# Attention probabilities transposed through device memory instead of on TensorE

## The chip, the cores and the metric

The kernel runs on one core of one Trainium2 chip. The metric is the device time of one execution in microseconds (us). Three executions of the kernel before gave 814.75, 814.80 and 814.91 us, median 814.8 us.

## What is computed

Two layers of a hybrid decoder trunk on 256 tokens of width 2048, all in float32. Each layer normalizes x, multiplies it with one wide input matrix (2048 x 6232), runs four mixers on the result, and multiplies their gated outputs with an output matrix (2048 x 2048):

```python
for l in range(DEPTH):
    h = _rmsnorm(x, ln_g[l])
    u = h @ w_in[l]
    y_a = _gla(...) * silu(g_a)
    y_b = _ssd_mixer(...)
    y_c = _mla(...) * silu(g_c)             # causal attention, 4 heads
    y_d = _dilated_attention(...) * silu(g_d)   # attention on dilated windows, 4 heads
    x = x + concatenate([y_a, y_b, y_c, y_d]) @ w_out[l]
```

The change concerns the two attentions, `mla` and `dil`. For each head: scores s = q k^T * scale with a mask, p = softmax(s), output p v. To multiply with v, TensorE needs the probabilities p with the keys on the partitions, and the softmax leaves them with the queries on the partitions: they have to be transposed.

## The kernel before

**The stream.** The large multiplications run as a stream of 148 units a layer: 144 units of two 128-row slabs of a weight block (`STREAM`, blocks of up to 512 columns, eight units each) and 4 projection units. Float32 weights are split into a high and a low float32r part. For each unit SP loads the weights into `raw` (four buffers, L530), ACT makes `w_hi` (L1019), DVE makes `w_lo` (L1384), and TensorE does 12 matmuls (hi x hi, hi x lo at L705 and L706, lo x hi at L714). `w_hi` and `w_lo` have four buffers each: ACT may split unit n once TensorE has finished unit n-4, and SP loads the weights of unit n once DVE has split unit n-4.

**The jobs.** The mixers' small TensorE work is put between the units. `PE_AT` names the unit behind which each job runs: `mla S 0: 89`, `mla PT 0: 92`, `mla S 1: 93`, `mla O 0: 94`, `mla PT 1: 96`, `mla O 1: 98`, `dil S 0: 99`, `dil PT 0: 102`, `dil S 1: 103`, `dil O 0: 104`, `dil PT 1: 106`, `dil O 1: 108`, `yT 3: 114`. The names `0` and `1` are pairs of heads. S is the scores, PT the transposition of the probabilities, O the product with the values. Jobs take turns on two halves of a PSUM tensor (`pairs`), and each waits for the last reader of the job two before it (`LAST_READER`).

**ACT and DVE** walk through the same units. At unit n each first does its split of unit n and then the work hung on that number: DVE takes the maximum of the scores at the unit of S plus 3 (`smax`, L1675, into `Pb`), ACT takes the exponential there (`probs`, L1221), then TensorE transposes `Pb` (`probs_T`, L899), ACT copies PSUM to `PT` (L1227), TensorE multiplies with the values (`values`, L910 to L912), and DVE scales the result by the sums (`out_heads`, L1707). For `dil` DVE also multiplies the probabilities with the tap counts (`taps`, L1687). The order of all signalling steps of each engine is written out in `ORDER`. A step that waits holds up everything behind it on its engine, the splits of later units too.

**Squares.** Seven other transpositions a layer (`SQUARES`: `ssd x`, `ssd y`, `dil q`, `dil k`, `y 0`, `y 1`, `y 2`) use no TensorE. DVE transposes 32 x 32 squares (`turn_squares`, L1353), one DMA writes the 512 KB to device memory (`squares_out`, L512), and when that has landed four DMAs read them back so that the squares take their new places (`squares_back`, L519). SP issues these DMAs in its queue among the weight loads, the first 5 units and the others 7 units behind the number in `SQUARES`. GpSimd does eight small reciprocal square roots a layer (`rsqrt`, L613 and L615) and four small loads.

Of the kernel before, what the change touches and what calls it, by code (L numbers as in the profile page):

```python
# [187 lines left out]
for _n in range(8):  # L188
# [3 lines left out]
          "mla kv 1": KV_AT, "ssd Y": 76, "mla qT": 85, "mla kT": 86, "mla rT": 87, "mla S 0": 89, "mla PT 0": 92,  # L192
          "mla S 1": 93, "mla O 0": 94, "mla PT 1": 96, "mla O 1": 98, "dil S 0": 99,
          "dil PT 0": 102, "dil S 1": 103, "dil O 0": 104, "dil PT 1": 106, "dil O 1": 108,
# [9 lines left out]
for _m in ("mla", "dil"):  # L204
    for _i in range(2):
        LAST_READER |= {f"{_m} S {_i}": ("dve", f"{_m} max {_i}"), f"{_m} PT {_i}": ("act", f"{_m} PT {_i}"),
                        f"{_m} O {_i}": ("dve", f"{_m} O {_i}")}
# [24 lines left out]
        "mla S 0, mla PT 0, mla S 1, mla O 0, mla PT 1, mla O 1, dil S 0, dil PT 0, dil S 1, dil O 0, "  # L232
        "dil PT 1, dil O 1, yT 3",
# [6 lines left out]
        "mla rT, mla P 0, ssd rs sum, mla PT 0, mla P 1, evac 11, mla PT 1, dil q, dil P 0, dil PT 0, "  # L240
        "evac 12, dil P 1, dil PT 1, yT 0, yT 1, yT 2, evac 13, yT 3",
# [8 lines left out]
        "mla nmax 0, dil q squares, dil k squares, mla max 1, mla nmax 1, y 1, mla ri 0, mla O 0, y 1 squares, y 0, y 0 squares, mla ri 1, mla O 1, dil max 0, "  # L250
        "dil nmax 0, dil P 0, dil max 1, dil nmax 1, dil P 1, dil ri 0, dil O 0, y 2, y 2 squares, yT 0, dil ri 1, dil O 1, yT 1, "
        "yT 2, y 3, yT 3, x turn 0, x turn 1, x turn 2",
# [7 lines left out]
def build(nc, xT_d, x_d, pos_d, cols_d, w_d, params_d, gla_w2, gla_b,  # L260
          consts_d, masks_d, out_d):
    ctx = ExitStack()
    with ctx:
# [117 lines left out]
        SQUARES["dil k"] = A(6656, 1024), A(6656, 1024), 93  # L381
# [69 lines left out]
        squares_d = {name: nc.dram_tensor(name.replace(" ", "_") + "_squares", (P, 4 * S), F32, kind="Internal").ap() for name in SQUARES}  # L451
# [55 lines left out]
        def _(sp):  # L507

            def squares_out(l, name):

                sp.wait_ge(*reached("dve", l)(f"{name} squares"))
                sp.dma_start(squares_d[name], SQUARES[name][0]).then_inc(squares_out_done[name], 16)  # L512

            def squares_back(l, name):

                sp.wait_ge(squares_out_done[name], 16 * (l + 1))
                away, to = squares_d[name].rearrange("(i b) (f c) -> f b i c", b=32, f=4), SQUARES[name][1]
                for f in range(4):
                    sp.dma_start(to[32 * f:32 * f + 32].rearrange("b (i c) -> b i c", i=4), away[f]).then_inc(squares_in[name], 16)  # L519
# [1358 lines left out]
```

## Time and profile before

| | us |
|---|---|
| median of three executions | 814.8 |
| profiled execution: its own time | 815.04 |
| profiled execution: span from first to last instruction | 813.2 |
| TensorE busy in it | 806.8 |
| DVE busy in it | 613.7 |
| ACT busy in it | 473.7 |
| share of the 16 DMA engines busy, mean | 64% |

The span is 1.8 us shorter than the execution's own time. Busy times overlap. The profile lists for each instruction its start, duration, source line and what ended the idle time before it; TensorE's unit boundaries are read off the start of the first L705 matmul of each unit.

### The profile page before, as it was taken

How to read it: one execution, taken by the hardware profiler on the slowest of the kernel's cores; microseconds unless marked ns; L12 is line 12 of the kernel's file. 1: busy time of each engine (PE TensorE's matmuls, PEld its weight loads, DVE VectorE, ACT ScalarE, POOL GpSimd, SP SyncE). 2: the span in 40 equal slices, each digit the busy share in tenths (PEclk: the TensorE clock that was granted, in tenths of full speed). 3: DMA queues.
4: the chain of work that ended last, by engine and by line, in shares of the span. 5: the costliest groups of instructions: out<-in, count | busy, mean ns of one | idle time of the engine just before them, and what ended most of it. 6: DMA issues, size and time to landing. Idle time of an engine off the chain costs nothing.

```text
span 813.2 us, 11261 instructions
## 1 busy us (share of the span) xinstructions
PE 806.8 (99%) x4164; PEld 684.3 (84%) x4164; DVE 613.7 (75%) x1092; ACT 473.7 (58%) x784; POOL 60.1 (7%) x64
## 2 busy tenths in 40 slices
PE   8999999999999999999999999999999999999998
PEld 5888887999887888888888888889998888888886
DVE  6678899877898766678964967979779977665452
ACT  6566544866965666433556465447687565664331
POOL 7100000110401000000000000003014010000000
PEclk9999999999999999999999999999999999999999
DMA  9956634586676967656576655355767677666553
GB/s 328 347 217 207 186 133 159 135 246 193 200 246 206 240 225 232 200 175 205 165 260 183 195 161 186 111 168 151 239 203 234 209 226 249 194 222 215 188 193 118
DMA packets 57687, 165.67 MB, mean 204 GB/s; under 512 B 6624, under 2 KB 14480, under 8 KB 57632
## 3 DMA queue, kind: packets, MB, share of 16 engines
q1 hardware_dynamic: 57120, 164.67, 63.9%
q8 instruction: 33, 0.54, 0.3%
q10 hardware_dynamic: 320, 0.21, 0.1%
q14 instruction: 22, 0.18, 0.1%
q0 software_dynamic: 192, 0.07, 0.1%
HBM read 155.47 MB, written 9.45 MB: 203 GB/s over the span
## 4 chain that ended last, share of the span: by engine, by line
PE 91%; DVE 6%; issue 2%; DMA 1%; ACT 0%; SPq 0%; DVEq 0%; ACTq 0%
PE gemm L705 27%; PE gemm L714 27%; PE gemm L706 26%; DVE arena L1345 3%; DVE w_lo L1384 2%; PE pairs L885 1%; PE pairs L855 1%; PE pairs L860 1%; PE pairs L856 1%; PE pairs L826 1%; PE pairs L771 1%; DVE arena L1473 1%; PE pairs L868 1%; PE pairs L899 1%; DMA u<-in_xT_dram 1%
## 5 line engine op out<-in xcount | busy, mean ns | idle before, releaser
L1384 DVE TENSOR_TENSOR w_lo<-raw,w_hi 128x1024 fp32r<-128x1024 f32 (+2 forms) x295 | 324.4, 1109 | 146.0 <-ACT w_hi L1019 144.3
L705 PE MATMUL gemm<-w_hi,a_hi 128*128 128x512 f32 (+1 forms) x1144 | 420.8, 373 | 0.3 <-ACT w_hi L1019 0.3
L706 PE MATMUL gemm<-w_hi,a_lo 128*128 128x512 f32 (+1 forms) x1144 | 414.3, 368 | 0.0
L1019 ACT ACTIVATE w_hi<-raw 128x1024 fp32r<-128x1024 f32 (+2 forms) x295 | 281.5, 968 | 214.1 <-PE gemm L714 137.0
L714 PE MATMUL gemm<-w_lo,a_hi 128*128 128x512 f32 (+1 forms) x1144 | 281.7, 368 | 0.2
L705 PEld LDWEIGHTS gemm<-w_hi,a_hi 128*128 128x128 f32 x1144 | 215.2, 188 | 36.4 <-issue 2.1
L706 PEld LDWEIGHTS gemm<-w_hi,a_lo 128*128 128x128 f32 x1144 | 215.2, 188 | 33.1
L714 PEld LDWEIGHTS gemm<-w_lo,a_hi 128*128 128x128 f32 x1144 | 203.2, 188 | 36.5 <-DVE w_lo L1384 1.9
L613 POOL TENSOR_TENSOR st<-st,powers 128x4 f32<-128x4 f32 (+2 forms) x8 | 10.1, 1263 | 429.5 <-ACT arena L1100 212.5
L1052 ACT ACTIVATE u<-gemm,st 128x512 f32<-128x512 f32 (+1 forms) x40 | 22.1, 603 | 15.8 <-PE gemm L714 15.8
L1221 ACT ACTIVATE arena<-arena,st 128x128 f32<-128x128 f32 (+1 forms) x32 | 13.1, 444 | 30.9 <-DVE st L1679 30.9
L1345 DVE STREAM_TRANSPOSE arena<-u 32x256 f32<-32x256 f32 x64 | 27.9, 436 | 1.2
L1345 DVE STREAM_TRANSPOSE u<-x 32x256 f32<-32x256 f32 x48 | 20.9, 436 | 0.6
L1554 DVE SCALAR_TENSOR_TENSOR u<-arena,allp,u 128x256 f32<-128x256 f32 x48 | 20.9, 473 | 0.0
L1202 ACT ACTIVATE arena<-u 128x192 f32<-128x192 f32 (+1 forms) x64 | 20.6, 335 | 0.0
L1644 DVE SCALAR_TENSOR_TENSOR u<-u,sth,param_rows 128x192 f32<-128x192 f32 (+1 forms) x64 | 19.9, 376 | 0.0
L1083 ACT ACTIVATE arena<-arena 128x256 f32<-128x256 f32 x16 | 6.8, 423 | 18.0 <-DVE arena L1445 18.0
L1675 DVE CUSTOM_DVE_ANT_0 arena<-pairs,cst 128x128 f32<-128x128 f32 (+1 forms) x32 | 9.5, 352 | 8.5 <-issue 3.5
L771 PEld LDWEIGHTS pairs<-arena 128*128 128x128 f32 x112 | 14.7, 191 | 1.2
L1513 DVE COPY_PREDICATED o<-lmask,pairs 128x512 f32<-128x512 uint8 x14 | 12.4, 886 | 4.2 <-issue 4.2
L1336 DVE SCALAR_TENSOR_TENSOR a_lo<-u,allp,a_hi 128x256 fp32r<-128x256 f32 x28 | 14.2, 552 | 1.6 <-ACT a_hi L1000 1.5
L771 PE MATMUL pairs<-arena 128*128 128x128 f32 x112 | 14.8, 275 | 0.0
(201 smaller groups left out, 623.3 us busy)
## 6 DMA issues: line engine op xcount, KB each, us to landing
raw<-in_weights_dram SPq DMA_DIRECT2D x225, 512.0 KB, 4.3
raw<-in_weights_dram SPq DMA_DIRECT2D x64, 278.0 KB, 3.1
y_squares<-arena SPq DMA_DIRECT2D x6, 512.0 KB, 6.0
arena<-y_squares SPq DMA_DIRECT2D x24, 128.0 KB, 3.9
raw<-in_weights_dram SPq DMA_DIRECT2D x6, 384.0 KB, 4.4
x<-in_x_dram SPq DMA_DIRECT2D x4, 512.0 KB, 6.2
o<-ssd_rows SPq DMA_DIRECT2D x8, 256.0 KB, 5.4
param_rows<-in_params_dram SPq DMA_DIRECT2D x2, 904.0 KB, 7.0
```

The source lines that it names most:

```text
L705: pe.matmul(acc_t[t], a_hi[:, k, tok[t]], hi, start=k == 0, stop=False)
L706: pe.matmul(acc_t[t], a_lo[:, k, tok[t]], hi, start=False, stop=False)
L714: last = pe.matmul(acc_ps[:, b % 2, t, 0:w], a_hi[:, k, t * P:(t + 1) * P], lo, start=False, stop=k == KT - 1)
L771: last = pe.matmul(to, W[:, p, t * P:(t + 1) * P], Ql[n % 2][:, :, t, p, :], start=True, stop=True)
L1019: A_(w_hi[:, g % SPLIT, 0:c], raw[:, g % RAW, 0:c], ACT.Copy).then_inc(hi_done, 1)
L1052: last = A_(u[:, t, c0 - N_GATE:c0 - N_GATE + w], acc_ps[:, b % 2, t, 0:w], ACT.Copy, scale=xrs[:, t:t + 1])
L1202: last = A_(sq[j % 8] if m == "mla" else sq[:, t, h, :], buf[:, t, 4 * i + h, :], ACT.Square, scale=buf.shape[-1] ** -0.5, accum_out=total ...
L1336: last = v.scalar_tensor_tensor(a_lo[:, k, :], part, gain(l, k), a_hi[:, k, :].bitcast(F32), ALU.mult, ALU.subtract)
L1345: last = v.transpose(to[32 * f:32 * f + 32, :, :, i, :], rows[32 * i:32 * i + 32, :, :, f, :])
L1384: TT(w_lo[:, g % SPLIT, 0:c], raw[:, g % RAW, 0:c], w_hi[:, g % SPLIT, 0:c].bitcast(F32), ALU.subtract).then_inc(split_done, 1)
L1554: last = STT(conv(f), xc[:, f, j:j + S], tap_weight(l, j, f), conv(f), ALU.mult, ALU.add)
L1644: last = STT(buf[:, t, 4 * i + h, :], buf[:, t, 4 * i + h, :], rs[:, j:j + 1], g, ALU.mult, ALU.mult)
```

## The change

The jobs `mla PT 0`, `mla PT 1`, `dil PT 0`, `dil PT 1` are gone from TensorE. The probabilities now take the way of the squares: DVE turns the 32 x 32 squares of `Pb` (two transposes of 128 x 384, the new `probs_squares`) into a part of `u` that the dil queries and keys have left, one DMA of 384 KB writes them out, four DMAs of 96 KB read them back to the same place, and ACT copies them to `PT` (`probs_T`). ACT does this copy one unit behind the number of the O job, and waits there for the data. The O jobs move from 94, 98, 104, 108 to 96, 101, 107, 111, and `dil S 0` and `dil S 1` from 99 and 103 to 98 and 102. `dil k squares` moves on DVE from unit 93 to 92, where `dil q squares` is; `mla P 0 squares` takes unit 93 and `mla P 1 squares` unit 97.

All DMAs of the squares, old and new, leave SP's queue for GpSimd's. There they stand in a written order between the `rsqrt` steps, and each `squares_back` is issued when its `squares_out` has landed.

```diff
-          "mla kv 1": KV_AT, "ssd Y": 76, "mla qT": 85, "mla kT": 86, "mla rT": 87, "mla S 0": 89, "mla PT 0": 92,
-          "mla S 1": 93, "mla O 0": 94, "mla PT 1": 96, "mla O 1": 98, "dil S 0": 99,
-          "dil PT 0": 102, "dil S 1": 103, "dil O 0": 104, "dil PT 1": 106, "dil O 1": 108,
+          "mla kv 1": KV_AT, "ssd Y": 76, "mla qT": 85, "mla kT": 86, "mla rT": 87, "mla S 0": 89,
+          "mla S 1": 93, "mla O 0": 96, "dil S 0": 98, "mla O 1": 101, "dil S 1": 102, "dil O 0": 107, "dil O 1": 111,
 ...
     "act":
-        "mla rT, mla P 0, ssd rs sum, mla PT 0, mla P 1, evac 11, mla PT 1, dil q, dil P 0, dil PT 0, "
-        "evac 12, dil P 1, dil PT 1, yT 0, yT 1, yT 2, evac 13, yT 3",
+        "mla rT, mla P 0, ssd rs sum, mla P 1, mla PT 0, evac 11, dil q, dil P 0, mla PT 1, "
+        "dil P 1, evac 12, dil PT 0, yT 0, yT 1, dil PT 1, yT 2, evac 13, yT 3",
     "dve":
-        "mla nmax 0, dil q squares, dil k squares, mla max 1, mla nmax 1, y 1, mla ri 0, mla O 0, y 1 squares, y 0, y 0 squares, mla ri 1, mla O 1, dil max 0, "
-        "dil nmax 0, dil P 0, dil max 1, dil nmax 1, dil P 1, dil ri 0, dil O 0, y 2, y 2 squares, yT 0, dil ri 1, dil O 1, yT 1, "
-        "yT 2, y 3, yT 3, x turn 0, x turn 1, x turn 2",
+        "mla nmax 0, dil q squares, dil k squares, mla P 0 squares, mla max 1, mla nmax 1, y 1, mla P 1 squares, y 1 squares, "
+        "mla ri 0, mla O 0, y 0, y 0 squares, dil max 0, dil nmax 0, dil P 0, dil P 0 squares, mla ri 1, mla O 1, "
+        "dil max 1, dil nmax 1, dil P 1, dil P 1 squares, y 2, y 2 squares, yT 0, dil ri 0, dil O 0, yT 1, "
+        "yT 2, dil ri 1, dil O 1, y 3, yT 3, x turn 0, x turn 1, x turn 2",
 ...
-        SQUARES["dil k"] = A(6656, 1024), A(6656, 1024), 93
+        SQUARES["dil k"] = A(6656, 1024), A(6656, 1024), 92
+
+        for _i in range(2):
+            SQUARES[f"mla P {_i}"] = SQUARES[f"dil P {_i}"] = (u[:, _i, COL["dq"]:COL["dq"] + 768],) * 2 + ((93, 97)[_i],)
 ...
         def _(sp):
 ...
-                    for name, (_, _, at) in SQUARES.items():
-                        if n == at + 5:
-                            squares_out(l, name)
-                        if n == at + 7:
-                            squares_back(l, name)
 ...
         def _(pool):
 ...
+            def squares_out(l, name):
+                pool.wait_ge(*reached("dve", l)(f"{name} squares"))
+                pool.dma_start(squares_d[name], SQUARES[name][0]).then_inc(squares_out_done[name], 16)
+            def squares_back(l, name):
+                pool.wait_ge(squares_out_done[name], 16 * (l + 1))
+                away, to = squares_d[name].rearrange("(i b) (f c) -> f b i c", b=32, f=4), SQUARES[name][1]
+                for f in range(4):
+                    pool.dma_start(to[32 * f:32 * f + 32].rearrange("b (i c) -> b i c", i=4), away[f]).then_inc(squares_in[name], 16)
 ...
                 rsqrt("mla crs", crs, css)
+                squares_out(l, "ssd x")
+                squares_back(l, "ssd x")
 ...
                 rsqrt("dil rs 1", drs[:, 8:16], dss[:, 8:16])
+                squares_out(l, "ssd y")
+                squares_back(l, "ssd y")
+                squares_out(l, "dil q")
+                squares_out(l, "dil k")
+                squares_out(l, "mla P 0")
                 rsqrt("ssd rs", brs, bss)
+                squares_back(l, "mla P 0")
+                squares_back(l, "dil q")
+                squares_back(l, "dil k")
+                for name in ("mla P 1", "y 1"):
+                    squares_out(l, name)
+                for name in ("mla P 1", "y 1"):
+                    squares_back(l, name)
+                for name in ("y 0", "dil P 0"):
+                    squares_out(l, name)
+                    squares_back(l, name)
+                for name in ("dil P 1", "y 2"):
+                    squares_out(l, name)
+                for name in ("dil P 1", "y 2"):
+                    squares_back(l, name)
 ...
                 def probs_T(m, i):
-                    act_.wait_ge(*pe(f"{m} PT {i}"))
-                    A_(PT[:, :, :], pair_of(f"{m} PT {i}")[:, :, 0:384], ACT.Copy).then_inc(*signal("act", f"{m} PT {i}"))
+                    act_.wait_ge(squares_in[f"{m} P {i}"], 16 * 4 * (l + 1))
+                    if (m, i) != ("mla", 0):
+                        act_.wait_ge(*pe(f"{m} O 0" if i else "mla O 1"))
+                    to, squares = PT.rearrange("p r (c i a) -> p i (r c) a", i=4, a=32), SQUARES[f"{m} P {i}"][1].rearrange("p (i x a) -> p i x a", i=4, a=32)
+                    A_(to, squares, ACT.Copy).then_inc(*signal("act", f"{m} PT {i}"))
 ...
-                            if n == slot(f"{m} PT {i}"):
+                            if n == slot(f"{m} O {i}", 1):
                                 probs_T(m, i)
 ...
+                def probs_squares(m, i):
+                    v.wait_ge(*(act if m == "mla" else me)(f"{m} P {i}"))
+                    if (m, i) == ("mla", 0):
+                        v.wait_ge(*me("dil k squares"))
+                    to = SQUARES[f"{m} P {i}"][0].rearrange("p (f r c a) -> p r f c a", f=4, r=2, c=3)
+                    for r in range(2):
+                        last = v.transpose(to[:, r], Pb[:, r].rearrange("p (c f b) -> p f c b", c=3, f=4))
+                    last.then_inc(*sig(f"{m} P {i} squares"))
```

## Rows read from the trace of the kernel before

**Rows 1.** The page: TensorE's busy time, and the chain that ended last, by engine.

```profile
PE 806.8 (99%) x4164; PEld 684.3 (84%) x4164; DVE 613.7 (75%) x1092; ACT 473.7 (58%) x784; POOL 60.1 (7%) x64
PE 91%; DVE 6%; issue 2%; DMA 1%; ACT 0%; SPq 0%; DVEq 0%; ACTq 0%
```

**Rows 2.** Timeline, PE, layer 0 (start us, us, engine line op): first matmuls of units.

```profile
250.30 0.39 PE L705 MATMUL gemm<-w_hi,a_hi 128*128 128x512 f32 x1
253.02 0.39 PE L705 MATMUL gemm<-w_hi,a_hi 128*128 128x512 f32 x1
256.31 0.48 PE L705 MATMUL gemm<-w_hi,a_hi 128*128 128x512 f32 x1
...
261.40 0.53 PE L705 MATMUL gemm<-w_hi,a_hi 128*128 128x512 f32 x1
...
265.58 0.48 PE L705 MATMUL gemm<-w_hi,a_hi 128*128 128x512 f32 x1
...
268.40 0.39 PE L705 MATMUL gemm<-w_hi,a_hi 128*128 128x512 f32 x1
...
274.51 0.39 PE L705 MATMUL gemm<-w_hi,a_hi 128*128 128x512 f32 x1
...
278.50 0.48 PE L705 MATMUL gemm<-w_hi,a_hi 128*128 128x512 f32 x1
...
282.44 0.58 PE L705 MATMUL gemm<-w_hi,a_hi 128*128 128x512 f32 x1
```

**Rows 3.** Line 899, the transposes of the probabilities (durations in ns: min/median/max).

```profile
L899 PE MATMUL pairs<-cst,arena x48: 270/272/273, 255.7 to 706.8; 128*128 128x128 f32 x48
```

**Rows 4.** Timeline, DVE, layer 0: maximum, dil squares, split, O 0 and gate.

```profile
249.56 0.28 DVE L1675 CUSTOM_DVE_ANT_0 arena<-pairs,cst 128x128 f32<-128x128 f32 x1
...
250.87 1.30 DVE L1353 STREAM_TRANSPOSE arena<-u 128x512 f32<-128x512 f32 x2
253.84 1.23 DVE L1384 TENSOR_TENSOR w_lo<-raw,w_hi 128x1024 fp32r<-128x1024 f32 x1 [1.67 <-ACT w_hi L1019]
...
267.15 1.13 DVE L1707 TENSOR_SCALAR o<-pairs,st 128x128 f32<-128x128 f32 x4
```

**Rows 5.** Timeline, ACT, layer 0: from the end of the first exponentials.

```profile
252.76 1.99 ACT L1019 ACTIVATE w_hi<-raw 128x1024 fp32r<-128x1024 f32 x2
...
257.21 0.79 ACT L1227 ACTIVATE arena<-pairs 128x768 f32<-128x768 f32 x1
...
268.60 1.27 ACT L1058 ACTIVATE arena<-gemm,st 128x512 f32<-128x512 f32 x2 [0.57 <-PE gemm L714]
269.88 1.28 ACT L1061 ACT_TABLE_LOAD   x1
...
272.83 1.05 ACT L1213 ACTIVATE fold<-arena 128x1024 f32<-128x1024 f32 x1
```

**Rows 6.** Issues of DMAs by tile: queue, count, KB each, median us from issue to landing.

```profile
dil_q_squares<-arena SPq DMA_DIRECT2D x2, 512.0 KB, 5.0
arena<-dil_k_squares SPq DMA_DIRECT2D x8, 128.0 KB, 7.6
out_dram<-x SPq DMA_DIRECT2D x1, 128.0 KB, 2.0
```

**Rows 7.** Line 519, reading squares back from SP, to landing; then line 619, GpSimd's 16 KB load.

```profile
DMA to landing us min/median/max: 2.7/4.3/9.5
...
DMA to landing us min/median/max: 2.8/3.8/4.9
```

**Rows 8.** Timeline, POOL: the issue of one DMA of 128 rows, and one of its tensor operations.

```profile
2.18 0.59 POOL L568 DMA_DIRECT2D cst<-in_consts_dram  x1
...
161.12 3.88 POOL L613 TENSOR_TENSOR st<-st,powers 128x4 f32<-128x4 f32 x1 [11.90 <-ACT arena L1169]
```

**Rows 9.** Stretches of 10 us: busy us of PE, PEld, DVE, ACT, POOL; clock; DMA share; GB/s.

```profile
252.00:262.00 10.00, 10.00 (x54) 7.97 (x53) 6.58 (x11) 6.95 (x17) 2.85 (x2) 1.00 0.61 190
262.00:272.00 10.00, 10.00 (x54) 8.52 (x53) 7.22 (x20) 8.42 (x15) 0.00 (x0) 1.00 1.09 246
```

## What the change will do to the time

> **What bounds the kernel now.** I read the page first, then TensorE's timeline over the attention stage, then ACT, DVE, the DMA issues and GpSimd in the same stretch. TensorE is busy 806.8 of 813.2 us and has 91% of the chain that ended last [rows 1]; it never stops in the attention stage, and its granted clock is 1.00 there, the 2.4 GHz level [rows 9]. So whatever is taken off TensorE's queue shortens the kernel by its full length, as long as nothing new makes TensorE wait. ACT and DVE are ahead of it by a lead that is worth nothing until it is used up.
>
> **Jobs taken away: the gain.** The unit starts give the price of a job. A plain unit takes 253.02 - 250.30 = 2.72 us. With the transposes behind it, it takes 256.31 - 253.02 = 3.29, so 0.57 for six transposes (each is listed at 272 ns [rows 3], but they overlap). The unit behind a job is 0.10 longer (268.40 - 265.58 = 2.82) [rows 2]. One job costs 0.67 us; eight of them, four a layer, 8 x 0.67 = 5.4 us. That all 48 transposes have 270 to 273 ns says that the eight jobs are alike [rows 3]. Moving S and O jobs costs TensorE nothing: the same matmuls behind other units, none of them sharing a unit before or after. If nothing waits, the profiled execution of 815.04 us becomes 809.7, and the median, 0.24 below it, becomes 809.4. That is the floor.
>
> **TensorE's new due times.** For the waits I need layer 0's clock without stalls. Other jobs, from [rows 2]: an O job 278.50 - 274.51 - 2.72 = 1.27; the two `mla` scores 261.40 - 256.31 - 2.82 = 2.27; `dil` scores 282.44 - 278.50 - 2.82 = 1.12; behind scores the next unit takes 265.58 - 261.40 - 1.27 = 2.91. Without PT 0, unit 93 starts at 255.74, unit 94 at 255.74 + 2.72 + 2.27 = 260.73, unit 95 at 263.64, unit 96 at 266.36, and **`mla O 0` is due at 269.08**. Then unit 97 at 270.35, unit 98 at 273.17, **`dil S 0` due at 275.89**, unit 99 at 277.01, units 100 and 101 at 279.92 and 282.64, **`mla O 1` due at 285.36**.
>
> **The first new chain, up to the data's return (call it T).** ACT has `mla P 0` at 252.76 [rows 5]. DVE does the maximum from 249.56 to 250.87, then `dil q` squares (two of 512 in 1.30) and now `dil k` squares at once, to 253.3. That costs nothing: its next split started only at 253.84 because it waited for ACT [rows 4]. That split ends at 255.0, and two transposes of 384 elements, three quarters of 1.30, end at 256.0. GpSimd issues the write at 256.1. SP's writes of 512 KB landed in 5.0 us [rows 6]; 384 KB is less, but GpSimd's path is slower: its 16 KB load took at least 2.8 us [rows 7] where SP's queue moved 128 KB in 2.0 [rows 6]. I take 5.3: landed at 261.4. The `ssd rs` step that stands between on GpSimd is short enough to fit in that wait. Four reads, 0.59 us of issue each [rows 8], so the last starts at 263.2; the median from issue to landing of such a read is 4.3 [rows 7], and with 0.3 for the slower path **T = 267.8**. Bounds: a write of 4.4 and the shortest read, 2.7 [rows 7], give 265.0; a write of 6 and the 7.6 that the `dil k` reads took [rows 6] give 271.5. The DMA engines are the reason for the upper end: in 262 to 272 they are full already (share 1.09, against 0.61 before that) [rows 9], with the `dil` reads in it. I stay near the lower half because the `dil` writes now start 3 us sooner, in engines that were idle, and GpSimd reads P 0 back ahead of `dil q` and `dil k`.
>
> The Trainium skill (DMA: Bandwidth & Descriptors, section "Anatomy of one DMA — SWDGE (gpsimd) path") fits one GpSimd DMA as 2.0 us plus bytes over 436 GB/s. As an estimate from that page, the write would take 2.9 us and a read 2.2, and T would be near 263, before anything waits. The trace speaks against using it here: already 16 KB took 2.8 to 4.9 us from GpSimd [rows 7].
>
> **What T sets.** `mla O 0` needs ACT's copy (0.8 for 768 elements [rows 5]): a stall of T - 268.2. But ACT now stands still at unit 97 from about 265.0 until T, with everything queued behind: the split of 98, the gate evacuation `evac 11` at 98 (table load, two activations, table load: 1.28 + 1.27 + 1.28), the split of 99, the `dil q` copy (1.05) [rows 5]. Starts lie about 0.1 closer than durations, so the split of 99 ends at T + 6.7 and the `dil q` copy at T + 7.7: `dil S 0` stalls by T - 268.2 too. DVE follows from T + 6.7: split of 99 1.13, sums and scaling of O 0 1.25, `y 0` 1.14, split of 100 1.14, `y 0` squares 1.22, split of 101 1.14, the maximum of `dil S 0` 1.31, together 8.3 [rows 4] (`y 0` priced as a split, which has the same 1024 elements). ACT then has `dil P 0` 1.5, the split of 102 0.95, and the copy for PT 1 0.8: T + 18.4. `mla O 1` is due at 285.36, so **it stalls by T - 267.0**. This is the tightest place, and the stalls don't add, since each delays the later due times too. With T = 267.8 a layer loses 0.8, with the handover some 0.9. Layer 1 repeats the pattern. Net: 809.4 + 2 x 0.9 = **811.2**.
>
> **The other new steps.** DVE gets four times 1.0 us of squares a layer. The first is hidden as shown; the second (unit 97) ends at 267.2 while DVE would wait for ACT; the `dil` ones lie behind `taps`, where DVE holds a lead of over 2 us before its next split is due. P 1: squares at 267.2, written behind the 12 reads of P 0, `dil q` and `dil k` on GpSimd (issued until 261.4 + 12 x 0.59 = 268.5), landed by 274, read back by about 281; wanted at T + 17.6 = 285.4: 4 us to spare. `dil k` back: last issued at 267.9, landed by 272.2 to 275.5, due 275.9. `dil P 0` and `dil P 1` have nine units, 24.5 us, from S to O for chains of about 18. The DMAs that leave SP's queue stood between weight loads; TensorE is without a pause there as it is [rows 9], so nothing is gained by that. The `ssd x` and `ssd y` reads come sooner or at the same time. `yT 3` was not late before, and O 1 moved to unit 111 leaves DVE three units, 8.2 us, for `dil O 1`, one split and the gate, about 5.
>
> **Rivals.**
> *No stall.* T is 267.0 or less, as the lower bound 265.0 allows: 809.4. For it: the DMA engines are idle when the writes start. Against: the slower GpSimd path. Chance 0.22.
> *Engines full.* The reads of P 0 share the engines with weights and take 6 us instead of 4.6, so T = 269.2 to 269.6 and a layer loses 2.5: the gain is given back, 814.4. Chance 0.13. For it: share 1.09 [rows 9].
> *DVE holds GpSimd off.* GpSimd's addition of 4 elements took 3.88 us once, with DVE at work on two-input operations without a pause [rows 8]. One such hold of 3 us between the write and the last read of P 0 gives T = 270.8, 3.8 a layer: 809.4 + 7.6 = 817.0. It decides from a hold of 1.8 us on. The Trainium skill (SBUF — State Buffer, section "SBUF: two separate sides") has a rule of this kind: while VectorE runs an operation that takes the shared port pair, GpSimd can't write descriptors, and a DMA issued from it waits. By that rule the time would be that of this rival. The trace supports it only with the one slow operation; the 0.59 us issue was taken at 2.18 us, before DVE had work of note, so it says nothing on this. Chance 0.15.
> *The issue itself is dear.* Against 0.59 [rows 8] each of GpSimd's issues for a rearranged read takes twice that. Then the chain over P 1 ends last: 12 reads to 275.6, two writes and their landing to 283, four reads and landing to 291, copy to 291.8, against 285.4: over 6 us less what P 0 already delayed, about 5.6 a layer: 820.6. It decides from about 0.9 us an issue. Chance 0.10.
> That the change doesn't do what it says (TensorE's queue not shorter) can be left out: the four jobs are gone from the code.
>
> **Numbers.** Forecast 811.2 with stalls of 0.3 to 1.8 us a layer (810.0 to 813.0), chance 0.40. Faster means below 813.2, slower above 816.4; 0.2% is about what a measurement of this kernel tells from no change. Faster: 0.40 + 0.22 = 0.62. Same: 0.13. Slower: 0.15 + 0.10 = 0.25. The range goes from a little below the floor, 809.0, to 817.5, which takes in the held-off GpSimd and leaves out the dear issue.
>
> **What would show it.** After the change TensorE's busy time and unit starts should show 2.72 at units 92, 96 (before the job), 102 and 106; a gap before the first L910 matmul of O 0 and O 1 in both layers, released by ACT's copy; ACT idle before the first copy from about 265 until T, released by a DMA. Wrong if TensorE waits for weight splits instead (then the engines were the limit), if T is before 267 (then 809.4), or if GpSimd's issue rows are far from 0.59 us.

## The result, and the profile after

| | us |
|---|---|
| before, on the same chip | 815.18 (814.62 to 816.7) |
| after | 818.68 (812.47 to 821.17) |
| ratio after / before | 1.0035 (95%: 1.0019 to 1.0051) |
| profiled execution after: its own time, span | 820.17, 818.0 |

The change made the kernel slower by 0.35%. The page of the kernel after, in the order of [rows 1], then its two DMA queues (packets, MB, share of the 16 engines):

```profile
PE 804.9 (98%) x4116; PEld 681.6 (83%) x4116; DVE 620.5 (76%) x1108; ACT 473.6 (58%) x784; POOL 118.6 (15%) x174
...
PE 72%; DMA 10%; DVE 10%; issue 3%; ACT 2%; POOL 2%; SPq 0%; DVEq 0%; ACTq 0%; POOLq 0%
...
q1 hardware_dynamic: 47040, 149.98, 57.6%
q0 software_dynamic: 7072, 21.05, 9.0%
```

TensorE has 48 matmuls fewer (4164 to 4116), as planned. But its share of the chain that ended last fell from 91% to 72%: the end is now reached over transfers. TensorE's timeline, layer 0, around `dil O 0` (L722 and L723 are the former L705 and L706, L918 is `values`):

```profile
301.74 0.39 PE L722 MATMUL gemm<-w_hi,a_hi 128*128 128x512 f32 x1
...
303.55 1.07 PE L731 MATMUL gemm<-w_lo,a_hi 128*128 128x512 f32 x4
307.73 0.49 PE L918 MATMUL pairs<-u,arena 128*128 128x128 f32 x2 [3.11 <-ACT arena L1234]
...
309.18 0.78 PE L722 MATMUL gemm<-w_hi,a_hi 128*128 128x512 f32 x1
...
311.03 0.63 PE L722 MATMUL gemm<-w_hi,a_hi 128*128 128x512 f32 x1
...
313.52 0.40 PE L722 MATMUL gemm<-w_hi,a_hi 128*128 128x512 f32 x1
```

TensorE stands for 3.11 us before `dil O 0`, released by ACT's copy at L1234. The unit with this job takes 309.18 - 301.74 = 7.44 us where an O job's unit takes 3.99 [rows 2]: 3.45 lost. The unit behind it takes 4.34 instead of 2.82, its matmuls 0.63 instead of 0.39: another 1.52. Two stretches around the stops (busy us of PE, PEld, DVE, ACT, POOL; clock; DMA share; GB/s):

```profile
302.00:312.00 10.00, 6.89 (x31) 5.54 (x30) 6.55 (x7) 4.63 (x5) 4.60 (x9) 0.85 0.84 258
710.00:720.00 10.00, 8.70 (x37) 7.55 (x38) 7.36 (x11) 7.25 (x8) 4.38 (x8) 0.83 0.96 294
```

Before, the attention stage had a granted clock of 1.00 [rows 9]; here part of each stretch runs at the lower of the two levels, 1.2 GHz, behind the stop. By the same unit starts, layer 1 loses 4.27 at its `dil O 0` (3.20 idle, and the job's own matmuls already slow) and 0.82 behind it, and `mla O 1` of layer 0 loses 0.60. Together 3.45 + 1.52 + 4.27 + 0.82 + 0.60 = 10.66. The profiled execution of before less the eight jobs is 815.04 - 5.36 = 809.68; with 10.66 it is 820.34, against 820.17 measured. Nothing else is needed to explain the time of this execution, one of the longer of the 20; the median is 1.5 below it.

Why ACT was late there: GpSimd's timeline (L594 is the write of `squares_out`, L601 the reads of `squares_back`), layer 0, then layer 1:

```profile
276.39 2.18 POOL L601 DMA_DIRECT2D arena<-y_squares  x4
279.92 0.56 POOL L594 DMA_DIRECT2D y_squares<-arena  x1 [1.35 <-DVE arena L1360]
288.10 2.18 POOL L601 DMA_DIRECT2D arena<-y_squares  x4 [7.62 <-DMA y_squares<-arena]
290.26 0.56 POOL L594 DMA_DIRECT2D dil_P_squares<-u  x1
300.14 2.18 POOL L601 DMA_DIRECT2D u<-dil_P_squares  x4 [9.31 <-DMA dil_P_squares<-u]
...
695.70 0.56 POOL L594 DMA_DIRECT2D dil_P_squares<-u  x1
704.22 2.18 POOL L601 DMA_DIRECT2D u<-dil_P_squares  x4 [7.96 <-DMA dil_P_squares<-u]
```

And the producer and the consumer, DVE's squares and ACT's copy:

```profile
284.86 1.04 DVE L1705 STREAM_TRANSPOSE u<-arena 128x384 f32<-128x384 f32 x2
306.84 0.84 ACT L1234 ACTIVATE arena<-u 128x768 f32<-128x768 f32 x1 [5.48 <-DMA u<-dil_P_squares]
```

The squares of `dil P 0` are ready at 285.9. Their write is issued at 290.26, 4.4 us later (6.7 in layer 1), because GpSimd first waits for `y 0`'s write and then issues `y 0`'s reads. From its issue until GpSimd may go on it takes 300.14 - 290.26 = 9.9 us, 8.5 in layer 1 (the landing itself is at 9.6 and 8.2), and the reads and their landing 6.7. From the end of `dil S 0` (276.46) to ACT's copy (306.84) the chain is 9.4 + 4.4 + 9.9 + 6.7 = 30.4 us long.

### The profile page after: what moved, and what is told of

Read it like the earlier page. It is cut to its first block, busy times and chain, and to the rows that moved or that the text cites. A ratio compares the mean times of both kernels' runs of the same rounds, so it can differ in the third digit from the quotient of the medians.

```text
span 818.0 us, 11223 instructions
## 1 busy us (share of the span) xinstructions
PE 804.9 (98%) x4116; PEld 681.6 (83%) x4116; DVE 620.5 (76%) x1108; ACT 473.6 (58%) x784; POOL 118.6 (15%) x174
## 2 busy tenths in 40 slices
DMA packets 54486, 171.94 MB, mean 210 GB/s; under 512 B 7264, under 2 KB 8464, under 8 KB 54432
## 4 chain that ended last, share of the span: by engine, by line
PE 72%; DMA 10%; DVE 10%; issue 3%; ACT 2%; POOL 2%; SPq 0%; DVEq 0%; ACTq 0%; POOLq 0%
PE gemm L722 22%; PE gemm L731 21%; PE gemm L723 21%; DVE w_lo L1391 3%; DVE arena L1352 3%; DMA dil_P_squares<-u 2%; DMA mla_P_squares<-u 2%; DMA y_squares<-arena 2%; POOL arena L601 1%; DMA u<-dil_P_squares 1%; POOL u L601 1%; DMA raw<-in_weights_dram 1%; PE pairs L877 1%; PE pairs L872 1%; PE pairs L873 1%
## 5 line engine op out<-in xcount | busy, mean ns | idle before, releaser
L722 PE MATMUL gemm<-w_hi,a_hi 128*128 128x512 f32 (+1 forms) x1144 | 421.5, 374 | 0.0
L723 PE MATMUL gemm<-w_hi,a_lo 128*128 128x512 f32 (+1 forms) x1144 | 415.3, 368 | 0.0
L722 PEld LDWEIGHTS gemm<-w_hi,a_hi 128*128 128x128 f32 x1144 | 216.2, 189 | 36.4 <-issue 1.5
L723 PEld LDWEIGHTS gemm<-w_hi,a_lo 128*128 128x128 f32 x1144 | 216.1, 189 | 33.7
L1352 DVE STREAM_TRANSPOSE u<-x 32x256 f32<-32x256 f32 x48 | 20.9, 436 | 0.6
L1561 DVE SCALAR_TENSOR_TENSOR u<-arena,allp,u 128x256 f32<-128x256 f32 x48 | 20.9, 473 | 0.0
L601 POOL DMA_DIRECT2D arena<-y_squares x24 | 13.1, 551 | 18.1 <-DMA y_squares<-arena 18.1
L788 PEld LDWEIGHTS pairs<-arena 128*128 128x128 f32 x112 | 14.7, 191 | 1.2
L1234 ACT ACTIVATE arena<-u 128x768 f32<-128x768 f32 x8 | 6.7, 838 | 15.5 <-DMA u<-dil_P_squares 11.8
```

Source lines behind the costliest of these rows:

```text
L601: pool.dma_start(to[32 * f:32 * f + 32].rearrange("b (i c) -> b i c", i=4), away[f]).then_inc(squares_in[name], 16)
L722: pe.matmul(acc_t[t], a_hi[:, k, tok[t]], hi, start=k == 0, stop=False)
L723: pe.matmul(acc_t[t], a_lo[:, k, tok[t]], hi, start=False, stop=False)
L788: last = pe.matmul(to, W[:, p, t * P:(t + 1) * P], Ql[n % 2][:, :, t, p, :], start=True, stop=True)
L1352: last = v.transpose(to[32 * f:32 * f + 32, :, :, i, :], rows[32 * i:32 * i + 32, :, :, f, :])
L1561: last = STT(conv(f), xc[:, f, j:j + S], tap_weight(l, j, f), conv(f), ALU.mult, ALU.add)
```

## Experiments

**Theory A**: the gain of the removed jobs is real, and it is lost because `dil P 0` stands behind `y 0` in GpSimd's queue: issued late, then landing late behind `y 0`'s reads, with a slow clock behind the stop on top. What speaks for something else is named in the expectations: the jobs were worth less, the new work of DVE and ACT costs time, GpSimd's queue is slow by itself, or the 16 engines are full whoever issues. "Before" in these comparisons was 815.26 to 815.53.

**The gain alone.** Before, without TensorE's transposes; ACT copies the probabilities as they are.

```diff
-                            last = pe.transpose(ps[:, r, c * P:(c + 1) * P], Pb[:, r, c * P:(c + 1) * P], ident)
...
-                    A_(PT[:, :, :], pair_of(f"{m} PT {i}")[:, :, 0:384], ACT.Copy).then_inc(*signal("act", f"{m} PT {i}"))
...
+                    A_(PT[:, :, :], Pb[:, :, 0:384], ACT.Copy).then_inc(*signal("act", f"{m} PT {i}"))
```

> The kernel before with TensorE's eight transposition jobs left out and everything else in its place: ACT copies the probabilities to PT as they are, not transposed, so the two attentions' values products are of the wrong operand. This prices the jobs alone. By my price of 0.67 us a job it runs 5.4 us under the kernel before, 809.5 to 810.0. If jobs overlapped with their neighbours, or if the four units of lead hid them, it would be nearer 813.

Measured: 809.48 (808.83 to 809.83), ratio 0.9928 (0.9915 to 0.9942). The eight jobs are worth 5.8 us; my sum said 5.4.

**The move of the queue alone.** Before, with its seven squares' DMAs on GpSimd.

```diff
-                        if n == at + 5:
-                            squares_out(l, name)
-                        if n == at + 7:
-                            squares_back(l, name)
...
+                squares_out(l, "dil q")
+                squares_out(l, "dil k")
                 rsqrt("ssd rs", brs, bss)
+                squares_back(l, "dil q")
+                squares_back(l, "dil k")
+                for name in ("y 1", "y 0", "y 2"):
+                    squares_out(l, name)
+                    squares_back(l, name)
```

> The kernel before with only the queue changed: its seven squares a layer go over GpSimd's queue, transposition of the probabilities stays on TensorE. Theory A (the loss is where the probabilities' round trip of dil heads 0 waits behind y 0's on GpSimd): no probabilities on this queue, so the time stays at 815.2, within 0.5. Theory B (GpSimd's way of issuing is itself the cost, through slower landings or by holding up the weight loads): slower, 817 or more, with gaps on TensorE before dil S 0 or in the splits.

Measured: 814.79 (814.51 to 815.82), ratio 0.9995 (0.9986 to 1.0005): free, and no gain.

**The changed kernel without the round trip of the probabilities.** DVE turns the squares and ACT copies them at once; the 384 KB write and its four reads are left out.

```diff
-                    act_.wait_ge(squares_in[f"{m} P {i}"], 16 * 4 * (l + 1))
+                    act_.wait_ge(*dve(f"{m} P {i} squares"))
```

> The changed kernel without the probabilities' way through device memory: ACT copies the squares to PT as soon as DVE has made them, so the 32 x 32 squares stay in their old places and both values products get a wrong operand; the eight writes and 32 reads of the probabilities are left out, all other work stays. Theory A (all that is lost is the wait for the probabilities' return): every gap before an O job goes but for the one that DVE sets at mla O 1 (0 to 0.5 us a layer): 809.5 to 810.5, clock 1.00. Theory B (DVE's squares, 1.0 us each, or ACT's copies also cost): 812 or more.

Measured: 809.61 (809.2 to 809.83), ratio 0.9928 (0.9915 to 0.9942). TensorE waits nowhere in the attention stage. DVE's squares, ACT's copies and the new places of the jobs cost nothing; all of the loss is in the round trips. This run can't tell the wait for their data from their load on the DMA engines, since it takes both away (165.64 MB moved instead of 171.94).

**`dil P 0` ahead of `y 0`'s reads.**

```diff
                 for name in ("y 0", "dil P 0"):
                     squares_out(l, name)
+                for name in ("dil P 0", "y 0"):
                     squares_back(l, name)
```

> The changed kernel with one order on GpSimd's queue changed: the write of dil P 0 is issued before the read of y 0 is waited for, and read back first. Theory A: the write is issued at about 286 instead of 290, lands before 296 instead of 300, the copy to PT is done before dil O 0 is due at about 304.5, the gap of 3.1 us in each layer goes and with it the fall of TensorE's clock behind it; 810 to 811.5 with all runs within 1 us. Theory B (the 16 DMA engines are full, whatever the order): the write takes as much longer, the gap stays at over 2 us, 816 or more.

Measured: 812.74 (811.5 to 814.12), ratio 0.9969 (0.9958 to 0.9981), clock 1.00. GpSimd's timeline of this kernel:

```profile
286.30 0.56 POOL L594 DMA_DIRECT2D dil_P_squares<-u  x1 [5.71 <-DVE u L1706]
289.41 2.21 POOL L601 DMA_DIRECT2D u<-dil_P_squares  x4 [2.55 <-DMA dil_P_squares<-u]
```

The write goes out 4 us sooner, GpSimd goes on after 3.1 us instead of 9.9, and the stop at `dil O 0` is gone. Exchanging the order of two steps brings 5.9 us; the 810 to 811.5 that was expected isn't reached. What is left over the floor is `mla O 1` (0.47 us idle) and `yT 3`, which waited for DVE 0.85 us in layer 0 and 1.65 in layer 1.

**`y 0`, `y 1`, `y 2` back on SP's queue, the probabilities alone on GpSimd's.** The same transfers as after, 171.94 MB. First SP's loop over the units, then GpSimd's list.

```diff
+                    for j, at in Y_TURN.items():
+                        if n == at + 5:
...
+                            sp.dma_start(squares_d[f"y {j}"], SQUARES[f"y {j}"][0]).then_inc(squares_out_done[f"y {j}"], 16)
+                        if n == at + 7:
...
+                                sp.dma_start(to[32 * f:32 * f + 32].rearrange("b (i c) -> b i c", i=4), away[f]).then_inc(squares_in[f"y {j}"], 16)
...
+                for name in ("mla P 1", "dil P 0", "dil P 1"):
                     squares_out(l, name)
                     squares_back(l, name)
```

> The changed kernel with the three y squares a layer back on SP's queue, 5 and 7 units behind their DVE step as before; GpSimd has the probabilities' alone, each written and read back at once. The same bytes. Theory A (a write issued behind other squares' reads on one queue waits for them): the writes of the probabilities land in 3 to 5 us instead of 6 to 10, no gap at dil O 0, 810 to 812. Theory B (full engines make the writes slow, whatever queue they are on): landings of 6 us and more stay, gap at dil O 0 0 to 2 us, 813 to 816.

Measured: **810.28** (809.63 to 811.33), ratio 0.9939 (0.9925 to 0.9952): faster than before and than after. GpSimd's timeline, and below it the stretch 285 to 305 of this kernel:

```profile
286.03 0.56 POOL L603 DMA_DIRECT2D dil_P_squares<-u  x1 [9.34 <-DVE u L1706]
289.14 2.18 POOL L610 DMA_DIRECT2D u<-dil_P_squares  x4 [2.55 <-DMA dil_P_squares<-u]
```

```profile
285.00:305.00 20.00, 19.84 (x99) 16.85 (x100) 15.78 (x37) 14.47 (x19) 5.48 (x10) 1.00 0.91 275
```

The same stretch after:

```profile
285.00:305.00 20.00, 19.29 (x92) 15.99 (x92) 15.78 (x37) 11.53 (x15) 6.02 (x11) 1.00 0.80 237
```

Over these 20 us the engines are fuller here (0.91 against 0.80), and GpSimd goes on 3.1 us after the write all the same. That doesn't clear the load of the 16 engines, because the two writes run at different moments. The stretch of the write itself, here and then after:

```profile
286.03:289.14 3.11, 3.11 (x18) 2.65 (x17) 3.11 (x4) 1.93 (x3) 0.56 (x2) 1.00 0.74 242
290.26:300.14 9.88, 9.88 (x46) 8.23 (x45) 6.03 (x24) 7.07 (x10) 0.57 (x2) 1.00 0.90 264
```

In layer 1 the share is 0.89 in both, with 3.2 us here and 8.5 after. But the reads that follow are slow here. Landings of `dil P 0` (KB each, median us from issue to landing), write and reads in this kernel, then the reads after:

```profile
dil_P_squares<-u POOLq DMA_DIRECT2D x1, 384.0 KB, 2.8
u<-dil_P_squares POOLq DMA_DIRECT2D x4, 96.0 KB, 7.7
...
u<-dil_P_squares POOLq DMA_DIRECT2D x4, 96.0 KB, 2.9
```

And the write of `dil P 1` takes 5.8 us in this kernel (6.8 in layer 1), with nothing issued on GpSimd's queue for 5.6 us before it; `dil P 0`'s own last read was still under way:

```profile
296.95 0.56 POOL L603 DMA_DIRECT2D dil_P_squares<-u  x1 [5.63 <-DVE u L1706]
302.78 2.18 POOL L610 DMA_DIRECT2D u<-dil_P_squares  x4 [5.27 <-DMA dil_P_squares<-u]
```

So what the move brought is read from the whole trip. From the squares of `dil P 0` ready to its last read landed it is 13.9 us here and 20.9 after (layer 1: 15.3 and 21.4). In layer 0, 4.1 of these 7.0 us come from the earlier issue, since GpSimd doesn't stand at `y 0`'s write any more, and 2.9 from a shorter trip. In layer 1 the earlier issue brings 6.4 and the trip is 0.3 longer.

**The write ahead of `y 0`'s reads.** GpSimd waits for `y 0`'s write as in the changed kernel and then issues `dil P 0`'s write before `y 0`'s reads.

```diff
+                squares_out(l, "y 0")
+                pool.wait_ge(squares_out_done["y 0"], 16 * (l + 1))
+                squares_out(l, "dil P 0")
                 for name in ("y 0", "dil P 0"):
-                    squares_out(l, name)
                     squares_back(l, name)
```

> The changed kernel, where GpSimd still waits for y 0's write to land, but then issues the write of dil P 0 before y 0's four reads instead of behind them. This moves the write by only 2.2 us. Theory A (a write issued behind reads on the same queue waits for them): it is issued at about 288.1 and lands in 3 to 4.5 us instead of 9.9, so that the data are back by 300 and the gap at dil O 0 is gone: 812 to 814, like the version with dil P 0 ahead. Theory B (only the lateness of the issue or the full engines count): it lands at 296 or later, a gap of 1 us or more stays in each layer, 815 or more.

Measured: 812.99 (811.87 to 816.05), ratio 0.9972 (0.9962 to 0.9983). Its GpSimd timeline:

```profile
287.88 0.56 POOL L594 DMA_DIRECT2D dil_P_squares<-u  x1 [7.47 <-DMA y_squares<-arena]
288.43 2.21 POOL L601 DMA_DIRECT2D arena<-y_squares  x4
294.55 2.18 POOL L601 DMA_DIRECT2D u<-dil_P_squares  x4 [3.91 <-DMA dil_P_squares<-u]
```

The write goes 2.4 us earlier (287.88 against 290.26), its reads 5.6 us earlier. GpSimd goes on after 6.7 us (5.3 in layer 1), between 3.1 and 9.9. The time is the expected one, the landing isn't: Theory A wanted 3 to 4.5. ACT still waits 1.10 us for the data (0.82 in layer 1), and TensorE no longer waits at `dil O 0`. With the write 2.4 us earlier as well as in front of the reads, the run doesn't separate the order from the moment.

**TensorE kept busy through the wait.** After, with 12 matmuls of 512 columns whose result nobody reads, in front of the wait at `dil O 0`.

```diff
-                    pe.wait_ge(*act(f"{m} PT {i}"))
...
+                    if (m, i) == ("dil", 0):
+                        for _ in range(12):
+                            pe.matmul(ps[:, 0, :], a_hi[:, 15, 0:P], a_hi[:, 8:10, :].rearrange("p k s -> p (k s)"), start=True, stop=True)
+                    pe.wait_ge(*act(f"{m} PT {i}"))
```

> The changed kernel with 12 matmuls of 512 columns, 2.7 us at the full clock, put in front of TensorE's wait at dil O 0 in each layer; their result is overwritten. If the fall of the granted clock (0.85 in 302 to 312 us, 0.83 in 710 to 720) comes from the idle time in front of it, TensorE is busy there now, the clock stays at 1.00, and the 1.5 and 0.8 us that the unit behind is too long go: 817.5 to 818.5, with less spread than 812 to 821. In runs in which the data come early it costs up to 5.4. If the clock falls for another reason, the time stays at 820 or goes up, clock still 0.995.

Measured: 816.37 (815.22 to 818.26), ratio 1.0014 (1.0005 to 1.0023). The stretches of before, now in this kernel:

```profile
302.00:312.00 10.00, 10.00 (x52) 8.50 (x51) 8.07 (x12) 4.75 (x5) 3.15 (x6) 1.00 0.89 292
710.00:720.00 10.00, 10.00 (x52) 8.49 (x51) 7.49 (x11) 4.81 (x6) 2.84 (x6) 1.00 1.00 261
```

With 5.4 us of work added, the kernel is 2.3 us shorter, more than was expected, and the clock stays at its upper level. The units behind the job take 2.82 us again, which gives back 1.52 + 0.82 = 2.3. That the median falls by just this is partly chance: the units with the job get shorter too (6.71 us in both layers instead of 7.44 and 8.25), and `yT 3` of layer 0 has a new stop of 1.57. The spread of the executions falls from 8.7 to 3.0 us. The changed kernel's own executions go the same way: those with a mean clock of 1.000 took 812.5 to 812.9 us, those at 0.994 took 820.6 to 821.2. How long TensorE stood in the short ones I can't say, since the profile is of one of the longer.

**`dil O 0` two units later** (109 instead of 107), so that the data may be late; DVE's scaling moves behind `yT 1` with it.

```diff
-"dil O 0": 107, "dil O 1": 111,
+"dil O 0": 109, "dil O 1": 111,
...
-        "dil P 1, evac 12, dil PT 0, yT 0, yT 1, dil PT 1, yT 2, evac 13, yT 3",
+        "dil P 1, evac 12, yT 0, dil PT 0, yT 1, dil PT 1, yT 2, evac 13, yT 3",
```

> The changed kernel with dil O 0 behind unit 109 instead of 107 (ACT's copy and DVE's scaling move with it), GpSimd's queue as changed. Theory A: the data of dil P 0 come at 306.8 in layer 0 and about 310.5 in layer 1 on the changed kernel's clock, dil O 0 is due 5.4 us later, at about 310, so the 3.1 to 4.3 us gap goes or leaves under 1 us; 811 to 812.5. Theory B (the engines are so full that the weights are late as well): new gaps at the units 108 to 115 in place of the old, 814 or more.

Measured: 818.39 (816.83 to 818.71), ratio 1.0032 (1.002 to 1.0045): no gain, where 811 to 812.5 was expected. TensorE's timeline, layer 0, and ACT's splits ahead of it:

```profile
329.48 1.97 PE L753 MATMUL pairs<-cst,o 128*128 128x128 f32 x8 [2.69 <-DVE o L1409]
...
309.00 1.06 ACT L1023 ACTIVATE w_hi<-raw 128x1024 fp32r<-128x1024 f32 x1 [3.66 <-DMA raw<-in_weights_dram]
313.74 1.06 ACT L1023 ACTIVATE w_hi<-raw 128x1024 fp32r<-128x1024 f32 x1 [3.69 <-DMA raw<-in_weights_dram]
```

The stops at `dil O 0` are gone, and in layer 0 a new one stands at `yT 3`; in layer 1 `dil O 1` (1.29 us) and `yT 3` (1.80) wait. In layer 0 ACT doesn't wait for `dil`'s probabilities at all. It waits for weights, whose loads take 7 to 10 us from issue to landing in this stretch (median after 4.3), and 1.83 us for `y 2`'s reads. In layer 1 it waits 4.93 us for weights, 3.58 for `dil P 1` and 1.30 for `y 2`. So the full engines of Theory B are seen here, and what stands late in GpSimd's queue adds to them.

**Both `dil` probabilities ahead**: as with `dil P 0` ahead, and `dil P 1` out and back before `y 2`.

```diff
                 for name in ("dil P 1", "y 2"):
                     squares_out(l, name)
-                for name in ("dil P 1", "y 2"):
                     squares_back(l, name)
```

> The kernel of the run with dil P 0 ahead of y 0, and dil P 1 now also read back before y 2's write is waited for. In that run a weight load landed 10 us late at 302 to 312 us beside dil P 1's and y 2's transfers, and yT 3 waited 1.65 us in layer 1. If the bunching of these transfers is the cause, reading dil P 1 back 4 us sooner spreads them: 811 to 812. If the total load of the engines is the cause, nothing changes: 812.7.

Measured: 817.06 (812.38 to 818.41), ratio 1.0006 (0.9992 to 1.002), where 811 to 812 was expected. GpSimd's timeline, and TensorE's in layer 1:

```profile
302.87 2.18 POOL L601 DMA_DIRECT2D u<-dil_P_squares  x4 [4.63 <-DMA dil_P_squares<-u]
305.04 0.56 POOL L594 DMA_DIRECT2D y_squares<-arena  x1
310.87 2.18 POOL L601 DMA_DIRECT2D arena<-y_squares  x4 [5.27 <-DMA y_squares<-arena]
```

```profile
730.07 1.65 PE L753 MATMUL pairs<-cst,o 128*128 128x128 f32 x8 [3.23 <-DVE o L1409]
```

Perhaps the same trap in another place: now `y 2`'s write stands behind the reads of `dil P 1` and takes 5.8 us (6.7 in layer 1), where it stood in front of them with `dil P 0` ahead only and took at most 4.3 (3.2). It was issued 0.5 us (1.5) earlier there, and the engines' share over it was 0.68 (0.67) against 0.98 (0.96) here, so this pair isn't clean either. `yT 3` waits 3.2 us in layer 1 and 1.2 in layer 0; in layer 1 ACT waited 5.87 us for `y 2`'s reads before that.

**All squares and probabilities on SP's queue**, at plus 5 and plus 7 units, as before (`mla` P at 93 and 97, `dil` P at 101 and 105). In SP's loop over the units:

```diff
+                    for name, (_, _, at) in SQUARES.items():
+                        if n == at + 5:
+                            squares_out(l, name)
+                        if n == at + 7:
+                            squares_back(l, name)
```

> The changed kernel without the change of queue: TensorE's jobs are gone and the probabilities take the way through device memory, but all squares are written 5 and read back 7 units behind their DVE step in SP's queue, as in the kernel before. Theory A (only the order on one queue made the loss; the weights' loads between the transfers keep them apart): no gap at dil O 0; mla P 1 comes back up to 2 us late for mla O 1, 810.5 to 813. If GpSimd's queue was needed (SP's waits for the writes hold the weight loads up, or the added bytes are too many for one queue): 815 or more, with ACT waiting for weights.

Measured: 831.63 (831.0 to 835.03), ratio 1.0212 (1.0197 to 1.0227), where 810.5 to 813 was expected. SP's queue, then ACT and TensorE:

```profile
260.33 1.85 SPq L520 DMA_DIRECT2D arena<-dil_q_squares  x4
262.23 1.85 SPq L520 DMA_DIRECT2D arena<-dil_k_squares  x4
264.12 0.43 SPq L531 DMA_DIRECT2D raw<-in_weights_dram  x1
264.60 1.85 SPq L520 DMA_DIRECT2D u<-mla_P_squares  x4
```

```profile
273.86 0.84 ACT L1218 ACTIVATE arena<-u 128x768 f32<-128x768 f32 x1 [9.22 <-DMA u<-mla_P_squares]
...
293.54 0.84 ACT L1218 ACTIVATE arena<-u 128x768 f32<-128x768 f32 x1 [2.03 <-DMA u<-mla_P_squares]
```

```profile
274.75 0.79 PE L902 MATMUL pairs<-u,arena 128*128 128x128 f32 x2 [5.97 <-ACT arena L1218]
...
294.43 0.49 PE L902 MATMUL pairs<-u,arena 128*128 128x128 f32 x2 [0.87 <-ACT arena L1218]
```

On one queue with the weights and behind the dilated reads, `mla P 0` is read at 264.60 instead of 260.94, its last read lands after 7.8 us instead of 4.2, and the data are back at 273.86, 7 us later than after. In layer 1 the stops are 6.68 and 0.65 us, and each unit behind a long stop is 1.0 to 1.1 us too long. `dil O 0` has no stop here. The run shows that putting everything on SP's queue in this order is worse; it changes the moments of the transfers too, and not the queue alone.

**`mla O 1` one unit later** (102), on top of the version with `y` on SP.

```diff
-"mla O 1": 101,
+"mla O 1": 102,
```

> The version with the y squares on SP's queue (810.3), with mla O 1 behind unit 102 instead of 101, in front of dil S 1. The 0.4 us gap at mla O 1 in layer 0 goes: 809.6 to 810.1. If the gap only moves to dil S 1's chain or to yT 3: 810.3 as before.

Measured: 810.49 (809.3 to 811.92), ratio 0.9941 (0.9929 to 0.9953): the same as without it, and not the 809.6 to 810.1 expected. In the profiled execution (809.3) the stop at `mla O 1` is gone and no other has come; 0.4 us is less than the executions differ among themselves.

## Why the prediction was wrong

*The jobs' price* held: 5.4 predicted, 5.8 measured without them. *The queue move and DVE's squares at no cost* held as well.

*The chain that I worked out in full* held. T was to be 267.8, with the write issued at 256.1; it goes out at 254.93, and ACT's copy starts after its wait at 266.9:

```profile
254.93 0.54 POOL L594 DMA_DIRECT2D mla_P_squares<-u  x1 [2.12 <-DVE u L1705]
...
266.89 0.84 ACT L1234 ACTIVATE arena<-u 128x768 f32<-128x768 f32 x1 [2.33 <-DMA u<-mla_P_squares]
...
284.44 0.83 ACT L1234 ACTIVATE arena<-u 128x768 f32<-128x768 f32 x1
```

The write took 5.4 us to land (5.3 forecast), the last read 4.2 (4.6). `mla O 0` has no stop, `mla O 1` one of 0.34 us in layer 0 and none in layer 1. My T + 17.6 for the second copy gives 284.5; it is at 284.44. By T alone the rival "No stall" (T of 267.0 or less) came true, but not its 809.4, since the loss arose elsewhere. The kernel with all on SP's queue tests the first formula with a late T: T - 268.2 is 5.7 (5.97 idle measured). That T - 267.0 = 6.86 also fits both stops together (5.97 + 0.87 = 6.84) is luck: the second copy should start at T + 17.6 = 291.5 and starts at 293.54, after a wait for its own data that the formula doesn't have, and the slow unit behind the first stop had moved the due time by 1.0.

*The step that failed* is "`dil P 0` and `dil P 1` have nine units, 24.5 us, from S to O for chains of about 18". The chain of `dil P 0` took 30.4. I never itemized the 18: the measured 9.4 up to the squares and the terms of T, 5.3 for the write and 6.4 for the reads, already make 21.1. I had the written order of GpSimd's queue, with `y 0` out and back before `dil P 0`, and walked it for `mla P 1` but not here: that is 4.4 us, 6.7 in layer 1. And I gave every transfer one landing time, whatever stood before it in its queue and however full the engines were: a write of 5.3 took 9.9, 8.5 in layer 1. The other side of the comparison was too short, and that hid part of it: from the end of `dil S 0` at 276.46 to the due time of `dil O 0`, 301.74 + 2.72 = 304.46, there are 28.0 us, since two jobs and the stop at `mla O 1` lie between the nine units. The chain with the copy took 307.73 - 276.46 = 31.3, so 3.3 of stop; the unit shows 3.45. As an estimate from these numbers, the late issue alone gives 21.1 + 4.4 + 0.9 for the copy = 26.4 in layer 0, still inside the 28.0: there it took the late issue and the slow write together.

*The clock* wasn't in the sum at all: 1.52 + 0.82 = 2.3 us of the loss in the profiled execution.

*The rivals.* "The issue itself is dear" falls: GpSimd's four reads take 2.18 to 2.25 us, 0.55 each. "DVE holds GpSimd off" falls too: in 285 to 305 DVE is busy for 15.78 of 20 us, and every issue there takes 0.55 to 0.56. The rule of the Trainium skill (SBUF — State Buffer, section "SBUF: two separate sides") on which that rival leaned isn't seen at work in this kernel; whether any of DVE's operations there takes the shared port pair isn't shown. "Engines full" was wrong where I put it, at `mla P 0`, whose last read took 4.2 us and not 6. At `dil P 0` it is neither shown nor refuted as part of the slow write. It isn't the whole cause, since the version with `y` on SP has fuller engines over the same 20 us and no stop there. My forecast that the kernel would lose a little at `mla O 1` in both layers was right in place for layer 0 and irrelevant in size.

*The fit of the Trainium skill* (DMA: Bandwidth & Descriptors, section "Anatomy of one DMA — SWDGE (gpsimd) path") gave 2.9 us for the write. I set it aside for 5.3. The first write of `mla P 0`, to which I applied it, took 5.4. The write of `dil P 0` landed in 2.8 us, as the fit has it, with `dil P 0` ahead and with `y` on SP's queue; after, it took 9.6. So the fit is met by the quickest landings of this kernel, and others take more than three times as long.

*Open*: how much of the slow write of `dil P 0` comes from `y 0`'s reads in front of it in GpSimd's queue, and how much from the weights and all else that the 16 engines move at that moment. For the order speaks `y 2`'s write, slower behind four reads than in front of them. For the moment speak `dil P 1`'s write and `dil P 0`'s reads in the version with `y` on SP, 5.5 to 10.2 us with none of `y`'s DMAs on their queue. No run holds the time of issue and changes only what stands in front. Why weight loads take 7 to 10 us in places was not pursued either. Some take 8 to 9.6 us in the kernel before too, without a stop; here they lie behind stops at `yT 3`, as in layer 1 with `dil P 0` ahead, where ACT waited 5.37 us for one.

## What to carry to other kernels

A queue of DMAs is a chain of its own: walk it step by step for each transfer that somebody waits for, with the waits of its neighbours, before giving that transfer a landing time. Where an engine waits for one round trip before it issues the next, put the write that is wanted first ahead of that wait, or give round trips that don't depend on each other to different issuing engines; here the same bytes took 818.7, 812.7, 810.3 or 831.6 us by queue and order alone. A stop of some 3 us on TensorE costs more than its length, through the clock behind it. And a fast write isn't a fast round trip: compare up to the last read's landing.

## What the runs showed of the hardware

- The same 384 KB write on GpSimd's queue landed in 2.8 to 9.6 us. It was 2.8 to 2.9 for `dil P 0`, in both layers, with `dil P 0` ahead or `y` on SP; 9.6 and 8.2 after, right behind four reads of 128 KB; 6.2 and 4.8 for `dil P 1` after, right behind four reads of 96 KB; and 5.5 and 6.6 for `dil P 1` with `y` on SP, with no new issue on its queue for 5.6 us. So no one landing time holds for a size, and neither the reads in front nor the share of busy engines orders these alone.
- The Trainium skill (DMA: Bandwidth & Descriptors, section "Issuing engines are not separate DMA queues") says that issuing from several engines only saves the time of issue, which is usually small. Here the time of issue holds GpSimd's wait for `y 0`'s landing, and moving `y` to SP's queue let `dil P 0`'s write go out 4.1 us (layer 1: 6.4) sooner after its squares: 8.4 us for the kernel. Whether the move also quickened the landings isn't shown: from issue to last landing it is 13.6 and 15.0 us instead of 16.6 and 14.7.
- The clock behind a stop. After a stop of TensorE of 1.29, 1.65 and 1.80 us the next plain unit took 2.84 to 2.86 us, as it does behind any job (2.82 to 2.93). After 2.69 us it took 3.51, after 3.11, 3.20 and 3.23 us it took 4.34, 3.64 and 3.98, with the granted clock at 0.83 to 0.85 in the 10 us around these stops, and after 5.97 and 6.68 us (all on SP) 3.84 and 3.88.
- Six fp32 transposes of 128 x 128 between two units cost the stream 0.67 us (unit starts) to 0.72 (5.8 us for eight jobs), though the profile lists 272 ns for each [rows 3]: listed durations of pipelined matmuls don't add.
